# One burst of value products per two chunks in a stick-breaking attention stage, with a longer ring of turned weights

## The reference

```
z = einsum('bthd,bshd->bhts', qb, kb)              # q already scaled by d ** -0.5
strict = arange(t1)[None, :] < arange(t0, t1)[:, None]
log_beta = log_sigmoid(z)
log_keep = where(strict, log_sigmoid(-z), 0.0)
after = cumsum(log_keep, axis=3, reverse=True) - log_keep
A = where(strict, exp(log_beta + after), 0.0)
out = einsum('bhts,bshd->bthd', A, vb)
```

## Time and profile before

| | |
|---|---|
| median of three runs | 3964.56 us |
| time of the profiled execution, its span | 3965.55 us, 3963.8 us |
| PE busy in the span | 3773.9 us (95%) |
| DVE busy | 2419.5 us (61%) |
| ACT busy | 1810.0 us (46%) |
| POOL busy | 766.3 us (19%) |
| mean granted PE clock | 0.977 of full speed |
| the attention's steps | 1857.9 to 3418.7 us |

### The profile page before, as it was taken

One profiled execution on the slowest core, in us unless ns is written; L12 is line 12 of the kernel. 1 busy time (PEld: TensorE's weight loads), 2 busy tenths in 40 slices (PEclk: granted clock), 3 DMA queues, 4 the chain that ended last, 5 costly groups with the idle time before them and its releaser, 6 DMA issues. The chain is left out here.

```text
span 3963.8 us, 66544 instructions
## 1 busy us (share of the span) xinstructions
PE 3773.9 (95%) x21459; PEld 2920.9 (74%) x21459; DVE 2419.5 (61%) x3264; ACT 1810.0 (46%) x3782; POOL 766.3 (19%) x594
## 2 busy tenths in 40 slices
PE   6399999999999999998999999999999999799998
PEld 2388878887887888775767676767676777588887
DVE  2578862323222111224898988898898899566665
ACT  2433321112122111213777776777677777455554
POOL 0212200002332231000121212121212121223322
PEclk8699999999999999998999999999999999899999
DMA  7752232225555443234120212121212120266554
GB/s 270 274 179 90 88 134 112 90 93 202 187 185 186 137 140 122 104 119 151 30 79 26 78 31 72 34 70 37 67 37 67 37 66 9 83 183 184 186 180 132
DMA packets 259511, 451.04 MB, mean 114 GB/s; under 512 B 32420, under 2 KB 139300, under 8 KB 252807
## 3 DMA queue, kind: packets, MB, share of 16 engines
q1 hardware_dynamic: 249464, 420.78, 32.2%
q0 software_dynamic: 9808, 27.28, 2.4%
HBM read 305.15 MB, written 147.00 MB: 114 GB/s over the span
## 5 line engine op out<-in xcount | busy, mean ns | idle before, releaser
L1086 DVE TENSOR_TENSOR_SCAN a_prod<-a_keep,a_prod,a_zeros 128x512 f32<-128x512 f32 x896 | 1136.7, 1333 | 117.6 <-ACT a_keep L1006 117.6
L1019 ACT COPY a_turned<-a_rt 128x512 f32<-128x512 f32 (+3 forms) x1152 | 656.5, 570 | 404.7 <-PE a_rt L932 388.7
L1006 ACT ACTIVATE a_keep<-a_z 128x512 f32<-128x512 f32 (+3 forms) x1152 | 685.8, 596 | 18.1 <-PE a_z L921 13.4
L932 PE MATMUL a_rt<-a_ident,a_prod 128*128 128x128 f32 x4224 | 666.7, 277 | 15.8 <-DVE a_prod L1086 9.7
L932 PEld LDWEIGHTS a_rt<-a_ident,a_prod 128*128 128x128 f32 x4224 | 494.9, 141 | 212.3 <-issue 83.9
L510 PE MATMUL p_bank<-p_hhi,p_whi 128*128 128x512 f32 (+1 forms) x1344 | 524.8, 390 | 35.2 <-DVE p_hlo L633 29.9
L948 PE MATMUL a_acc<-a_turned,a_dw 128*64 128x256 f32 (+1 forms) x4352 | 532.6, 379 | 0.0
L920 PE MATMUL a_z<-a_khi,a_q 128*128 128x512 f32 (+1 forms) x1144 | 525.3, 459 | 7.6 <-issue 5.0
L510 PE MATMUL p_bank<-p_hlo,p_whi 128*128 128x512 f32 (+1 forms) x1344 | 524.1, 390 | 0.0
L510 PE MATMUL p_bank<-p_hhi,p_wlo 128*128 128x512 f32 (+1 forms) x1344 | 524.0, 390 | 0.0
L948 PEld LDWEIGHTS a_acc<-a_turned,a_dw 128*64 128x64 f32 x4352 | 291.3, 136 | 195.6 <-issue 63.7
(11 more groups left out here) (210 smaller groups left out, 4732.2 us busy)
## 6 DMA issues: line engine op xcount, KB each, us to landing
p_hraw<-scratch_hT SPq DMA_DIRECT2D x42, 2048.0 KB, 7.8
n_xt<-in_x SPq DMA_DIRECT2D x8, 2048.0 KB, 11.0
scratch_hT<-n_hout SPq DMA_DIRECT2D x8, 2048.0 KB, 7.4
a_khi<-scratch_skh SPq DMA_DIRECT2D x128, 128.0 KB, 2.9
a_klo<-scratch_skl SPq DMA_DIRECT2D x128, 128.0 KB, 3.0
m_xt<-in_x SPq DMA_DIRECT2D x32, 512.0 KB, 4.0
out_y<-m_ot SPq DMA_DIRECT2D x32, 512.0 KB, 2.9
n_wada<-in_w_ada SPq DMA_DIRECT2D x4, 2048.0 KB, 15.3
```

What stands on the lines that cost most here:

```text
L932: last = pe.transpose(rt[k % RB][:, i * P:(i + 1) * P], prod[:, n % PB, i, q * P:(q + 1) * P], ident[:])
L1006: act.activation(keep[:, k % KB, 0:w], z[k % ZB][:, 0:w], ACT.Sigmoid, scale=-Z_SCALE).then_inc(keep_done, 1)
L1019: act.copy(turned[:, k % TB, t:], rt[k % RB][:, t:]).then_inc(turned_done, 1)
L1086: dve.tensor_tensor_scan(prod[:, n % PB, q, 0:w][:, ::-1], keep[:, k % KB, 0:w][:, ::-1], zeros[:, 0:w], first, ALU.mult, ALU.add).then_in ...
```

## The change

The bursts of two chunks stand behind one another after every second chunk: after chunks 2, 4, ... 34 instead of after each of chunks 1 to 34. The two last bursts of a head stay where they are. Since a chunk now waits up to a chunk longer for its burst, the ring `turned` gets 12 tiles (three chunks), and the count that its writer waits for is moved by one (AV0). A row can be added up only behind a later burst, so `row_out` moves: `out_step` puts it 2 steps into the first chunk behind the burst that ends the row. That is one step later than before where the last chunk of the row has an odd number and five where it is even: k = 38, 70, 94, 110, 126, 142 for rows 0 to 5 in place of 37, 65, 89, 109, 125, 137. Rows 6 and 7 stay at the end of the head (k = 143).

```diff
-    TB = 2 * TPC
+    TB = 3 * TPC
...
-        KEEP0, SCAN0, RT0, TURN0, AV0, SUM0 = ZB, KB, TPC * PB, RB, 2, 2
+        KEEP0, SCAN0, RT0, TURN0, AV0, SUM0 = ZB, KB, TPC * PB, RB, 3, 2
+
+        def out_step(r):
+            n = row_last[r] // TPC
+            return min(TPC * (n + 2 + (n + 1) % 2) + 2, N - 1)
...
-                    if 0 < n < NC - 1:
+                    if n and n % 2 == 0:
+                        weigh(n - 2)
                         weigh(n - 1)
...
                     for r in range(NCH):
-                        if min(row_last[r] + TPC + 2, N - 1) == k and r < NCH - 1:
+                        if out_step(r) == k and r < NCH - 1:
                             row_out(r)
```

## The result

| | before | after |
|---|---|---|
| median of the runs (us) | 3966.01 (3962.25 to 3967.8, 6 runs) | 3982.99 (3981.41 to 3985.43, 6 runs) |
| profiled execution, its span | 3963.8 | 3980.5 |
| mean granted clock | 0.977 | 0.970 |
| ratio after / before, 95% | | 1.0044 (1.0032 to 1.0055) |

What follows compares the result with a forecast made beforehand. PE alone paces from a head's fourth chunk to its end, DVE the passage between heads. Sum: -40.0 (merges) + 31.8 (passages) + 2.4 (end) + 2 (tight places) = -3.8 us, so about 3961 us, range 3938 to 3980.

Steps and rivals of the forecast that it cites:

- A merged burst: Inside the heads: joining two bursts saves 0.31 us (bounds 0.27 and 0.37); 129 merges gain 40.0 us.
- Rival C: Bursts do not join; each new weigh costs what the mode change does, nothing is gained: 4001 us, chance 0.05.
- The new wait: Between heads: sum(7) waits for store(5), which shares its buffer, and starts at 13.5 in place of 9.37 us.
- The jump: Between heads: DVE leaves its loop jump 3.37 us after sum(7), in series with the wait; first scan at 17.6.
- Rival A: Between heads: the jump's 3.37 us overlap the wait for the store, 20 us less: 3941 us, chance 0.25.
- The third chunk: New head's third chunk on PE: starts 3.7 us later at a typical passage; weigh(0) behind it adds 1.3 us.
- PE's wait for the scans: Sign in the changed profile: this wait grows from 35.6 us by about 7 x 5.
- The passages in sum: Seven passages from head to head: 4 x 5.0 + 2 x 3.7 + 4.4 = 31.8 us lost.
- The end of the stage: Last head: sum(5) about 3.3 us later, then four POOL pieces in a row: 2.4 us lost (1.7 to 3.0).
- The tight places: Inside heads: even chunks after a row with POOL's split, scans barely in time: 0.25 us per head, 2 in all (0 to 16).
- Rival B: Inside heads: the rings run out and ACT's 0.96 us per step paces PE: 3988 us, chance 0.15.
- in head 0 alone: A head's first merge pays only where PE paces, so only in head 0, at 0.31 us a merge.

Runs made afterwards that it cites:

- the second experiment: Kernel before with only the rows' additions moved to the later steps (142 for row 5), bursts single, ring of eight tiles: 4000.89 us, ratio 1.0096.
- the first experiment: Changed kernel with a buffer of its own for row 7's sum, so sum(7) waits for no store of the same head: 3944.26 us, ratio 0.9952.
- the fillers: Changed kernel with 52 more useless identity transposes on PE per head, 28 before the second chunk's last scores, 24 before the third chunk: 3976.77 us, ratio 1.0033.

## Why the prediction was wrong

**What bounds the kernel: right.** PE paces inside the heads, DVE the passages. The gain stands in the first and the loss in the second, and each experiment moved only its own: 171.07 us within a head in the second experiment, 166.55 in the first.

**A merged burst: right, a little small.** (171.07 - 166.55) / 16 = 0.28 us a merge, where I took 0.31 with bounds 0.27 and 0.37. The 0.27 from whole chunks was the better reading; the 0.37 summed holes, one of them up to the end of a record, and the ends of PE's records are modelled. Over the eight heads 36.3 us are gained instead of 128 x 0.31 = 39.7: 3.4 of the miss. Rival C is refuted by the row of x32.

**The new wait: right in mechanism, 4.2 us short in all.** sum(5) ended at t = 6.10 (predicted 6.05), weigh(35) started at 6.15 (6.15), and the profile names the store. But sum(7) started at 14.4 to 14.8 in the six passages with a jump, not at 13.5; only the last one, at 13.56, met it. The failed step is "store(5) is issued at 6.05 + 4.9 = 10.95 and lands at 13.5": at these six the store goes out 5.3 to 6.0 us after sum(5), and sum(7) starts 2.6 to 3.0 behind that instead of 2.5. SP's seven loads now fall into the time in which PE and ACT are at the jump, and the pair on a_khi takes 1.6 to 2.1 us instead of 1.19; at the last passage, which has no jump, the pair takes 1.18 and the store goes out after 4.90. What slows SP there I did not try. The first scans came at 18.3 to 19.0 instead of 17.6.

The third chunks are 26.9 us later in all, against 4 x 3.7 + 2 x 2.4 + 3.1 = 22.7 predicted: 4.2 of the miss. That is a difference of two errors. The six with a jump lose 6.2 us more than predicted, the last one 2.0 less (1.1 instead of 3.1), since the 1.7 us that I had put there for POOL beside the scans did not come. The scans of that passage ran at full speed, 12 in 14.20 us, and it was POOL's operation that became long (lengths on POOL are rough):

```profile
3250.56 14.20 DVE L1091 TENSOR_TENSOR_SCAN a_prod<-a_keep,a_prod,a_zeros 128x512 f32<-128x512 f32 x12
...
3250.89 14.70 POOL L875 TENSOR_TENSOR a_osum<-a_osum,a_v_e 64x512 f32<-64x512 f32 x1 [1.13 <-DVE a_osum L1102]
```

**The jump: right.** DVE restarted 3.2 to 3.5 us after sum(7) at the six, and at once at the last. Rival A, that the jump overlaps the wait, is refuted by six of six passages, and by the first experiment, where the sum comes 6 us earlier and so does the jump (3.36 us behind the sum in the passage shown; at the other five the scan started 0.12 us after ACT's keep, which came last there).
The Trainium skill (Advanced Engine Details and Errata, Control Flow Timing) has 108 ns for a compare-and-branch; the 3.36 us of the first experiment, where no store is waited for, show a jump that takes far longer than that.

**The third chunk: wrong, and this is the step that failed most.** I put 6.9 us on it (5.6 plus 1.3 for weigh(0) behind it), 39.4 + 9.1 = 48.5 in all. The first experiment and the fillers have just this: 6.92 and 6.87. The changed kernel took 8.3 to 9.7: its granted clock was at the lower level, after PE had idled for 2.67 and 1.62 us just before, in the rows of PE above. I counted idle time of PE as lost once, at its own length, and not what it does to the work behind it: 61.6 - 48.5 = 13.1 us, the largest part of the miss. The signs were there in the kernel before: the PE stalls of 1.3 us at the passages 2 to 3 and 4 to 5, which I took from the earlier trace rows as given and called "PE stalls", are the only two half-clock spans among its steps. The sign that the prediction named, PE's wait for the scans grown by about 35 us, did not come either (32.6 against 35.6).
The Trainium skill (TensorE: Matmul & The Clock Gate, HAM oscillation) warns of idle time between bursts that throws the clock back again and again. I did not weigh that rule, and it speaks against this change; the fillers' row agrees that idle time is what counts. The waits in the page's own example are longer than the 2.67 and 1.62 us here.

**The passages in sum.** +49.1 measured against 31.8 predicted: 4.2 up to the third chunks' start, 13.1 from the clock behind it.

**The end of the stage: right.** +2.0, predicted 2.4 (1.7 to 3.0).

**The tight places: no cost.** The rings never ran out; two full chunks take 3.66 + 7.30 = 10.96 us, within the 10.94 to 10.99 that I named. From the fourth chunk on the smallest slack between a chunk's last scan and its transposes was 0.3 us at chunk 34, and 1.7 elsewhere. Rival B is refuted, and with it the 2 us that I had set aside. In their place the first chunks of head 0 took 1.1 more than before, where 0.3 less was predicted, and the rest of the program 0.7 more: 2.1 off the forecast. Of head 0 the trace shows the cause. Before, PE waited there twice for loads from memory:

```profile
1859.10 0.49 PE L920 MATMUL a_z<-a_khi,a_q 128*128 128x512 f32 x1 [0.54 <-DMA a_dw<-scratch_dw]
...
1864.16 0.50 PE L920 MATMUL a_z<-a_khi,a_q 128*128 128x512 f32 x1 [0.90 <-DMA a_dw<-scratch_dw]
```

In the changed kernel it waits three times, 2.8 us in all:

```profile
1860.24 0.49 PE L924 MATMUL a_z<-a_khi,a_q 128*128 128x512 f32 x1 [0.68 <-DMA a_dw<-scratch_dw]
...
1865.53 0.49 PE L924 MATMUL a_z<-a_khi,a_q 128*128 128x512 f32 x1 [1.28 <-DMA a_dw<-scratch_dw]
...
1870.20 0.49 PE L924 MATMUL a_z<-a_khi,a_q 128*128 128x512 f32 x1 [0.80 <-DMA a_dw<-scratch_dw]
```

The failed step is "in head 0 alone" the first merge pays: the loads set the time there, and weigh(0), which used to stand ahead of the third chunk, no longer covers part of the wait. What the other 0.7 us are no run shows.

From -3.8 to the +16.6 of the table: 3.4 (merges), 4.2 (the third chunks' start), 13.1 (clock) and 2.1 (head 0 and the rest), less 2.0 and 0.4 (the tight places and the end), is 20.4. No rival had the clock in it. The measured 3982.99 is nearest to rival B's 3988, by luck: the slower side of the range, which ended at 3980, was made of rings that run out, a mechanism that was not there. The place to look was the one that the forecast itself named as losing 32 us.

## What to carry to other kernels

Where a delay makes TensorE wait, price it twice: once for the delay itself, and once for the clock of the work behind it. Look for the second in the trace that you already have, at the places where its present stalls are longest. When an instruction moves later, ask whose buffer it releases: here one sum that moved by five steps held back the sum of the row that shares its buffer, and through DVE's one queue the whole next head. A change that is good in the long steady phase need not be made at its ends: leaving two bursts single at either end of each head turned 17 us lost into 33 gained.

## What the runs showed of the hardware

- After idle stretches of PE of some 2.6 us, with others near them, at a passage in a stage where PE is otherwise busy for 98%, the granted clock fell to half for 3.4 to 6.8 us at a time, ten times in the changed kernel. With 52 small transposes per head in the holes it was full in the third chunk of every passage; half clock was left (20.4 us in all) only ahead of it.
- A jump back of the head's loop costs DVE 3.0 to 3.6 us before its next instruction, in series with the instruction before it, wherever nothing else came later; without a jump it is 0 to 0.4.
- SP's issue of the same loads takes longer while PE and ACT are at that jump: 1.6 to 2.1 us for a pair that takes 1.18 at the same kernel's passage without a jump.
- DVE's scans and POOL's additions slow each other, and either can be the one that waits: POOL's addition took 14.70 us beside scans that ran at their usual 1.18 us each, and in the kernel before 1.95 us at the same passage, beside scans of 2.0 to 2.2.
- A burst of half-width products right behind another costs 0.28 us less than one between full-width transposes, and a change of accumulator between the two costs nothing that the trace shows. That the 0.28 us are the price of changing the width and back is not shown; no run has the change without the burst.
